# Two transformer blocks on one core: the norms of the last two heads taken by chunk ahead of the inverse of the delta rule, the next pair's factors turned a level later, and key results copied first

## The reference

```python
qkv = jax.nn.silu(causal_depthwise_conv(qkv, conv_w))
q, k, v = jnp.split(qkv, [GDN_KDIM, 2 * GDN_KDIM], axis=-1)
q = l2_norm(heads(q, GDN_DK))     # x * rsqrt(sum(x * x) + EPS), 8 heads of 128
k = l2_norm(heads(k, GDN_DK))

# gated_delta_rule, by chunk
q = q * dk ** -0.5
decay = jnp.exp(jnp.where(incl, g_cum[..., :, None] - g_cum[..., None, :], -jnp.inf))
k_beta = k * beta[..., None]
a_low = jnp.where(strict, jnp.einsum('bhncd,bhnsd->bhncs', k_beta, k) * decay, 0.0)
rhs = jnp.concatenate([v * beta[..., None], k_beta * jnp.exp(g_cum)[..., None]], axis=-1)
sol = lax.linalg.triangular_solve(eye + a_low, rhs, left_side=True, lower=True, unit_diagonal=True)
attn_intra = jnp.einsum('bhncd,bhnsd->bhncs', q, k) * decay
```

## Time and profile before

| | |
|---|---|
| median of 3 executions | 2322.6 us (2318.1 to 2330.74) |
| profiled execution | 2318.65 us, span 2316.8 us |
| mean granted clock of the PE | 0.935 of full speed |
| busy over the span | PE 88%, DVE 45%, ACT 31%, POOL 15% |
| projection and inverse in the span | 697 to 953.4 us and 953.7 to 1130.5 us |

### The profile page before, as it was taken

How to read it: one execution, slowest core, us unless ns; L and a number is a source line. 1 busy time by engine, 2 the same in 40 slices (tenths; PEclk the granted TensorE clock), 3 DMA queues, 4 the chain that set the end, 5 groups by cost and what they waited for, 6 DMA issues and landing times. The chain is left out here.

```text
span 2316.8 us, 28906 instructions
## 1 busy us (share of the span) xinstructions
PE 2038.6 (88%) x11212; PEld 1508.8 (65%) x11212; DVE 1035.5 (45%) x1493; ACT 710.1 (31%) x1118; POOL 343.9 (15%) x311
## 2 busy tenths in 40 slices
PE   5988894987767999598999999997898779999999
PEld 2766662322226777377877888885676557888887
DVE  3432434111126578646445344334497654544333
ACT  2422132110113444243324222232442653322222
POOL 1332011111112443134221000000000321000000
PEclk9999896998988999789999999998899889999999
DMA  8146026999951222000012322321221002222321
GB/s 332 51 151 235 11 73 272 376 424 423 418 234 73 91 82 91 19 2 2 2 55 77 105 91 100 96 95 55 82 75 62 0 18 84 98 94 97 99 100 46
DMA packets 61950, 283.32 MB, mean 122 GB/s; under 512 B 9984, under 2 KB 11296, under 8 KB 52512
## 3 DMA queue, kind: packets, MB, share of 16 engines
q1 hardware_dynamic: 53072, 266.95, 31.2%
q0 software_dynamic: 6256, 11.03, 1.3%
q10 hardware_dynamic: 2528, 4.01, 0.5%
HBM read 280.90 MB, written 14.68 MB: 128 GB/s over the span
## 5 line engine op out<-in xcount | busy, mean ns | idle before, releaser
L307 PE MATMUL ps<-ff_hhi,ff_whi 128*128 128x512 f32 x704 | 276.7, 393 | 8.6 <-DVE ff_hlo L2662 8.3
L308 PE MATMUL ps<-ff_hhi,ff_wlo 128*128 128x512 f32 x704 | 275.4, 391 | 0.0
L309 PE MATMUL ps<-ff_hlo,ff_whi 128*128 128x512 f32 x704 | 275.3, 391 | 0.0
L2580 DVE TENSOR_TENSOR ff_wlo<-ring,ff_whi 128x1024 fp32r<-128x1024 f32 x132 | 163.6, 1239 | 247.4 <-ACT ff_whi L2576 247.4
L2576 ACT ACTIVATE ff_whi<-ring 128x1024 fp32r<-128x1024 f32 x132 | 139.3, 1055 | 321.5 <-PE ps L309 300.0
L1451 PE MATMUL ps<-w_up,hgT 128*64 128x512 f32 x576 | 144.6, 654 | 45.9 <-DMA w_up<-experts 45.9
L307 PEld LDWEIGHTS ps<-ff_hhi,ff_whi 128*128 128x128 f32 x704 | 133.2, 189 | 38.3 <-DVE ff_wlo L2580 10.2
L308 PEld LDWEIGHTS ps<-ff_hhi,ff_wlo 128*128 128x128 f32 x704 | 133.1, 189 | 28.0 <-issue 0.5
L309 PEld LDWEIGHTS ps<-ff_hlo,ff_whi 128*128 128x128 f32 x704 | 133.0, 189 | 28.0
L307 PE MATMUL ps<-ff_ahi,ff_whi 128*128 128x512 f32 x352 | 136.9, 389 | 0.0
L308 PE MATMUL ps<-ff_ahi,ff_wlo 128*128 128x512 f32 x352 | 136.9, 389 | 0.0
(11 more groups left out here) (543 smaller groups left out, 3949.1 us busy)
## 6 DMA issues: line engine op xcount, KB each, us to landing
ring<-stream SPq DMA_DIRECT2D x276, 512.0 KB, 3.3
w_up<-experts SPq DMA_DIRECT2D x36, 2048.0 KB, 17.7
mix<-experts SPq DMA_DIRECT2D x18, 1024.0 KB, 20.9
hn<-experts SPq DMA_DIRECT2D x18, 1024.0 KB, 21.8
yrow<-y_dram SPq DMA_DIRECT2D x4, 1024.0 KB, 8.0
tab<-table POOLq DMA_DIRECT2D x1, 2528.5 KB, 12.3
res<-xT ACTq DMA_DIRECT2D x1, 2048.0 KB, 18.5
h_dram<-mix SPq DMA_DIRECT2D x4, 512.0 KB, 11.1
```

Of the source, the lines that this page charges most:

```text
L307: pe.matmul(out, w_hi, a_hi, start=start, stop=False)
L308: pe.matmul(out, w_lo, a_hi, start=False, stop=False)
L309: return pe.matmul(out, w_hi, a_lo, start=False, stop=stop)
L2580: ve.tensor_tensor(w_lo[:, j % 2, :], ring[:, (B0 + j) % SLOTS, :], w_hi[:, j % 2, :].bitcast(F32), ALU.subtract).then_inc(blocks_done, 1)
```

## The change

1. In the projection the last pair's four `sums`, `roots` and `normalise` go. In their place `late_sums` makes the sums of the squares by chunk: 16 matmuls, each with 128 x 4 weights that are one in one column, so that chunk c has its four rows (q6, k6, q7, k7) at PSUM partitions 32c to 32c + 3 of bank 2. `late_roots` takes four roots of 4 x 128 into `late`, a part of `sml`. Two constants are set on POOL early in the block.
2. In the inverse the DVE inverts `late` (128 x 128) behind its two memsets. Behind the first pair's `spread_rows` the PE spreads the rows of `late` over all partitions (`late_rows`, 16 matmuls with 4 rows and 128 columns), and behind the first pair's `difference` the DVE scales Q and K of heads 6 and 7 in eight operations of 128 x 256. `decays` and what follows on the DVE stand behind them, `pair_products` on the PE behind `late_rows`.
3. `turn_t` of the next pair moves from behind level 4 to behind level 5, ahead of `turn_kv`.
4. `keep_result` copies K's result first. The next pair's level 1 waits for K's copy ahead of its first half and for V's ahead of its second half.

```diff
         rows = tab[0:8, TABLES["rcount"]].rearrange("p (a t) -> p a t", a=4)
+        late, late_eps = sml[:, 2 * T:2 * T + P], sml[:, 2 * T + P:2 * T + P + 1]
+        hot = TABLES["hot"].start + 7
...
-                turns(pe, one_turn, lambda before: [sums(u, before) for u in range(2)])
+                def late_sums(before):
+                    pe.wait_ge(conved[0], before * 3 + 3)
+                    for n in range(4):
+                        pe.wait_ge(squared[n // 2], before * 2 + n % 2 + 1)
+                        for c in range(TT):
+                            m = pe.matmul(ps[32 * c:32 * c + 4, 2, 0:P], tab[:, hot - n:hot - n + 4],
+                                          sq[:, n // 2, n % 2, c * P:(c + 1) * P], start=n == 0, stop=n == 3)
+                    m.then_inc(late_sum, 1)
+                turns(pe, one_turn, late_sums)
...
                 for n in range(4):
                     rest_of_block(0, n)
+                pool.memset(late[:, :], 1.0).then_inc(late_set, 1)
+                pool.memset(late_eps[:, :], EPS).then_inc(late_set, 1)
...
-                turns(act, one_turn, lambda before: [roots(u, before) for u in range(2)])
+                def late_roots(before):
+                    act.wait_ge(late_set, 2)
+                    act.wait_ge(late_sum, 1)
+                    for c in range(TT):
+                        r = slice(32 * c, 32 * c + 4)
+                        act.activation(late[r, :], ps[r, 2, 0:P], ACT.Sqrt, bias=late_eps[r, :]).then_inc(late_root, 1)
+                turns(act, one_turn, late_roots)
...
-                turns(ve, one_turn, lambda before: [normalise(u, before) for u in range(2)])
+                turns(ve, one_turn, lambda before: None)
...
                         if lv == 1:
                             pe.wait_ge(S["t_copy"][u], p + 1)
-                            if p:
-                                pe.wait_ge(S["fin_kept"][u], 2 * p)
+                            if p == 0:
+                                pe.wait_ge(late_done, 4 * u + 4)
+                            else:
+                                pe.wait_ge(S["fin_kept"][u], 2 * p - 1)
...
                             if lv > 1:
                                 pe.wait_ge(S["tT_up"][u], TUPS * p + lv - 1)
+                            elif p:
+                                pe.wait_ge(S["fin_kept"][u], 2 * p)
...
+                def late_rows():
+                    pe.wait_ge(late_inv, 1)
+                    for c in range(TT):
+                        r = slice(32 * c, 32 * c + 4)
+                        for n in range(4):
+                            a = 32 * c + n
+                            m = pe.matmul(ps[:, 4 * (c // 2) + 2 + c % 2, n * P:(n + 1) * P],
+                                          tab[r, a:a + 1].to_broadcast([4, P]), late[r, :], start=True, stop=True)
+                        m.then_inc(late_back, 1)
                 both = range(2)
-                for part in (spread_rows, pair_products, turn_t, turn_kv):
+                for u in both:
+                    spread_rows(0, u)
+                late_rows()
+                for part in (pair_products, turn_t, turn_kv):
...
-                    beside = {1: spread_rows, 3: pair_products, 4: turn_t, 5: turn_kv} if p + 1 < NPAIR else {}
+                    beside = {1: (spread_rows,), 3: (pair_products,), 5: (turn_t, turn_kv)} if p + 1 < NPAIR else {}
...
-                    for n, keep in enumerate((V, K)):
+                    for n, keep in ((1, K), (0, V)):
...
-                for part in (difference, decays, read_products, first_level, keep_kd):
+                ve.reciprocal(late[:, :], late[:, :]).then_inc(late_inv, 1)
+                for u in range(2):
+                    difference(0, u)
+                for c in range(0, TT, 2):
+                    ve.wait_ge(late_back, c + 2)
+                    for n in range(4):
+                        x = (Q, K)[n % 2][:, HEADS - 2 + n // 2, c * P:(c + 2) * P].rearrange("p (b t) -> p b t", b=2)
+                        ve.scalar_tensor_tensor(x, x, (P ** -0.5, 1.0)[n % 2],
+                                                ps[:, 2 * c + 2:2 * c + 4, n * P:(n + 1) * P], ALU.mult, ALU.mult
+                                                ).then_inc(late_done, 1)
+                for part in (decays, read_products, first_level, keep_kd):
```

More of the change, by code:

```diff
@@ L1558, in program @@
         egl = sb("egl", [P, HEADS, TT], on=gdn)
+        late, late_eps = sml[:, 2 * T:2 * T + P], sml[:, 2 * T + P:2 * T + P + 1]
+        late_set, late_sum, late_root = (sem(f"late_{n}") for n in ("set", "sum", "root"))
+        hot = TABLES["hot"].start + 7
         rows = tab[0:8, TABLES["rcount"]].rearrange("p (a t) -> p a t", a=4)
@@ L1980, in program @@
         zeroed = sem("i_zeroed")
+        late_inv, late_back, late_done = (sem(f"late_{n}") for n in ("inv", "back", "done"))
         NPAIR = HEADS // 2
@@ L2085, in _ @@
                 for p in range(NPAIR):
-                    beside = {1: spread_rows, 3: pair_products, 4: turn_t, 5: turn_kv} if p + 1 < NPAIR else {}
+                    beside = {1: (spread_rows,), 3: (pair_products,), 5: (turn_t, turn_kv)} if p + 1 < NPAIR else {}
                     for lv in range(1, LEVELS + 1):
                         level(p, lv)
-                        if lv in beside:
+                        for part in beside.get(lv, ()):
                             for u in both:
-                                beside[lv](p + 1, u)
+                                part(p + 1, u)
                     for u in both:
```

## The result

| | before | after |
|---|---|---|
| median | 2321.66 us (20 executions, 2315.23 to 2342.57) | 2302.17 us (20 executions, 2296.55 to 2319.99) |
| ratio of times | 1 | 0.9917, 95% interval 0.9894 to 0.994 |
| profiled execution | 2318.65 us, span 2316.8 | 2312.3 us, span 2310.5 |
| mean granted clock | 0.935 | 0.934 |

The change saves 19.5 us by the medians, 19.3 by the ratio (13.9 to 24.6); 17.0 were forecast. So the whole spans of two profiles are not compared here; the stretch from the first record of the sums to the next stage's first matmul is, and parts of it.

The account below looks back on a forecast made before the run. Holes in the PE's row, not transfers, were taken to bound the kernel. -16.7 + 7.6 - 7.9 + 0 = -17.0 gave 2301.6 us on the profiled execution, 2305.6 with 3.95 for the median; range 2298 to 2313.

Parts of the forecast that it names:

- Part 1: Projection's tail: late sums and roots replace the old sums, roots, reciprocals and scalings; gain 16.7 us, bounds 14.3 to 17.0.
- Part 2: Inverse, first pair: late rows and multiplications ahead of the decays make them 7.6 us later; bounds 0.6 to 8.2.
- The choice of half clock: First pair's spreads and late rows: PE at 1.2 of 2.4 GHz, so late rows take 7.2 us instead of 3.8.
- Part 3: Inverse, three pairs: factors turned behind level 5 remove the PE's 2.14 us hole; gain 7.9 us, bounds 5 to 9.
- first_level ends at 1053.76 ... just in time: Pair 1: VectorE's first_level ends at 1053.76, level 5's first subtraction is due at 1053.7, so no wait.
- Rival (d): Inside level 5, VectorE's first_level becomes the wait and the turn's move gives nothing; gain 9.1, 2313.5 us; chance 0.07.
- An idle PE put down to VectorE: Sign of being wrong: the PE idles inside level 5, waiting for VectorE; no size given.
- late rows of 7 us and decays at 16: Signs of being right in the first pair: late rows take 7 us, decays start 16 us after the PE's start.
- Part 4: Pair's end, K copied first: ScalarE's four copies are the chain; gain 0, bounds 0.1 lost to 1.5 us gained.
- (a): Low ends meet: serial sums with table load behind, 8.2 back, 5 from the turn; gain 11.1, 2311.5 us; chance 0.15.
- (b): Clock stays up over spreads and late rows: cost 0.6 to 4.2 instead of 7.6; 2298.6 to 2302.2 us; chance 0.15.
- (c): Inverse's clock recovers later: nine more half-clock levels eat the gain, fifteen make it over 12 us slower; chance 0.03.

Follow-up runs that it names:

- sums in turn: Changed kernel with the late sums done chunk by chunk, so that eight records of one column group follow one another; one execution, 2315.80 us.
- the repeat: Changed kernel measured and profiled again, unedited; median 2303.07 us of 6, ratio 0.9915 to the kernel before.
- the part alone: Kernel before with only K's result copied first, and the waits that go with it; one execution, 2318.84 us.
- three and four edits: Changed kernel with GpSimd's level 6 masks held, late rows across row groups, scaling behind decays: 2298.04 us; with V copied by VectorE too: 2294.14, again 2297.94.
- the late norms alone: Changed kernel with the factors' turn back behind level 4 and V copied first again; median 2305.71 us of 10, ratio 0.9938.
- POOL's wait: Changed kernel with GpSimd's level 6 masks held until the next pair's first_level is done; median 2301.0 us of 10, ratio 0.9938.

## Why the prediction was right

**Part 1** was forecast at 16.7 and measured at 16.70. The sums at 1.1 us (1.06) held. That the table load stands behind the two waits is not settled by after, where ScalarE was busy with a silu until 953.03 and both waits were over by then; the row of the sums in turn shows it. Here it cost nothing either way. The four roots took 1.51 against 1.4.

**Part 2** was forecast at 7.6 and measured at 4.6 to 5.0 for the decays, 3.6 and 5.6 for level 1. The choice of half clock was right: 0.52 over spreads and late rows. The mis-sized term is the late rows: 0.224 each was a quarter of a 512-column spread; a record of 4 rows and 128 columns took 0.155, the 32 together 4.97 instead of 7.2. Another 0.7 is that the rows start 6.52 us after the first spread and not 7.2, and the last four multiplications came to 969.02 - 967.65 = 1.4, counted from the rows' end (962.68 + 4.97), against 1.5; together that makes decays at 12.86 instead of 15.9.

**Part 3** was forecast at 7.9. At equal clock pairs 1-2 gained 1.0, of which 0.9 is the turn; from level 5's start to the transposes of K it was 5.95 us (1056.71 - 1050.76) instead of 4.55 forecast. If these 1.40 are missing in each of three pairs, 7.9 - 4.2 = 3.7 are left; that is the forecast corrected, not a measurement. The step that failed is "first_level ends at 1053.76 ... just in time". It took that end from the trace of before, where VectorE had the time to itself. In before, GpSimd was idle just then: the PE was at the factors' turn, so level 5's first product, which GpSimd's masks for level 6 wait for, came late:

```profile
1050.50 1.28 POOL L2155 TENSOR_TENSOR Q<-Q,inv_er 128x512 f32<-128x512 f32 x1
...
1051.93 0.86 DVE L2213 TENSOR_TENSOR inv_tT<-inv_aT,tab 64x256 f32<-64x256 f32 x2
...
1052.83 0.17 DVE L2216 COPY egl<-inv_er 128x4 f32<-128x4 f32 x1
...
1055.07 2.14 POOL L2163 TENSOR_TENSOR inv_bmT<-hctx,tab 128x512 f32<-128x512 f32 x2 [3.28 <-PE ps L2006]
```

With the factors' turn behind level 5, that product follows level 4 at once, GpSimd starts at 1051.49 instead, and its masks and the scaling of Q behind them lie exactly beside `first_level`. VectorE's slowed steps end 0.27 and 0.02 us after GpSimd's. The move of one PE step thus moved another engine's work onto the step that the PE waits for. The trace of before had shown the price, in the first pair, where both engines run side by side:

```profile
970.88 1.20 POOL L2163 TENSOR_TENSOR inv_bmT<-inv_aT,tab 128x512 f32<-128x512 f32 x1 [1.09 <-DVE inv_aT L2205]
972.04 2.92 POOL L2155 TENSOR_TENSOR Q<-Q,inv_er 128x512 f32<-128x512 f32 x2
972.39 1.12 DVE L2216 COPY egl<-inv_er 128x4 f32<-128x4 f32 x1
...
976.17 0.17 DVE L2216 COPY egl<-inv_er 128x4 f32<-128x4 f32 x1
```

The same copy, 1.12 beside GpSimd and 0.17 without. I had not compared these lines. (The Trainium skill, "GPSIMD Engine Reference", Specifications, says that GpSimd shares its SBUF interfaces with VectorE and contends with its instructions in a 2-port mode or with two SBUF inputs. The trace agrees: the two-input step went from 0.86 to 2.45.)

Rival (d), that `first_level` becomes the wait inside level 5, came true in its mechanism and not in its price: it took back a half of part 3, not all. An idle PE put down to VectorE was also a sign of being wrong that the prediction had named, and it was there (1.26); late rows of 7 us and decays at 16, named as signs of being right, were not.

**Part 4** was forecast at 0 and brought 0.1 a pair, by the repeat and by the part alone. That ScalarE is the chain was half right: with two of its copies gone only 0.4 came free.

**The sum.** The stage is 21.5 shorter than before in the first profile and 14.9 in the repeat; 2.0 of the difference is in level 1, 4.5 in the stretch behind it. It goes with the clock: by the brackets, the PE was at half from the first spread to pair 2's level 6 for 44.9 us in before, 34.1 in the first profile and 51.2 in the repeat. On a straight line between the two profiles, 44.9 us would give 17.3, an estimate from three executions. By parts, 16.7 - 5.6 + 3.7 + 0.3 = 15.1 with the repeat's level 1, whose 5.6 has 9.1 us more at half clock in it. By the whole kernel's ratios, part 1 with part 2 is worth 14.4 (forecast 9.1) and part 3 4.9 (forecast 7.9), each known to some 6 us only, together the 19.3 of the change.

The median's 19.5 lies between the two stages' 14.9 and 21.5; what a usual execution gains in the stage is open. Some 4 us of it may lie in unchanged stages: behind the stage the 14 profiled executions spent between 1180.0 and 1185.6 us, before 1184.3 and both of after 1180.2, and one profile of before can't tell a lasting difference from chance. So the forecast of the total was near for parts that erred both ways: part 2 too dear by 2 to 4, part 3 too good by 4.2. That these nearly cancelled was luck; only part 1 was right to its steps.

Rivals (a), (b) and (c): sums in turn cost 1.1 and not the 2.4 that (a) wanted; the clock did not stay up (b), though the PE's pause was 3.4 us; and (c), a later recovery, came in one profile and small: from the first spread to pair 0's level 6 the clock was at half for 34.7 us in before, 27.3 in the first profile and 44.4 in the repeat. By the 6.6 us that 17.1 us more at half clock made between the two profiles, these 9.7 cost an estimated 4, not the 17 that (c) wanted.

## What to carry to other kernels

When a step is moved, list what it released and what its new neighbour releases on every engine: here a PE step moved by one level, and GpSimd's masks came to lie on VectorE's step that the PE waits for. Take a duration from a row with the same neighbours, and look in the trace for the same instruction with another duration; that is what contention looks like before it is tried. And where the clock falls and rises within a stage, compare distances with equal time at half clock, not stage totals.

## What the hardware showed that was not expected

**A busy PE at half clock for some 38 us.** The first block's attention (L802 to L828), far ahead of the change and the same code in both kernels, by stretches, first before, then the first profile of after:

```profile
235.00:275.00 40.00, 37.50 (x314) 28.53 (x314) 13.74 (x21) 6.73 (x14) 1.80 (x1) 0.88 0.06 16
```

```profile
235.00:275.00 40.00, 37.88 (x246) 34.17 (x248) 7.49 (x17) 1.97 (x6) 1.80 (x1) 0.52 0.05 16
```

The groups by line in 240 to 280, again before and then after (line, engine, operation, names, shapes, count | busy us, mean ns | idle):

```profile
L822 PE MATMUL ps<-qb,SS 64*128 64x64 f32 x128 | 9.0, 280 | 0.0
```

```profile
L822 PE MATMUL ps<-qb,SS 64*128 64x64 f32 x128 | 15.8, 424 | 0.0
```

The PE was busy for 37.88 of 40 us at a mean clock of 0.52. The seam of this execution comes at 951.73 instead of 932.59, and the kernel with sums in turn, whose clock there was 0.58, has it at 946.96. In the other twelve profiles the sums start between 932.6 and 937.4. This accounts for the long profiled execution of after: against the repeat the seam is 17.7 later (934.04 there) and the stage 6.6 shorter, 11.1 of the 11.2 us between the two; that it also makes the long ones among the unprofiled executions of either kernel is likely from their distance of some 15 us, not shown. (The Trainium skill, "TensorE: Matmul & The Clock Gate", Part 1, has the clock rise with a busy PE; this stretch disagrees.)

**The clock in the pairs.** Each pair's spreads bring half clock for 3.4 or 6.8 us. All profiles of the kernels with three and four edits have 6.8 in both pairs. That costs 1.6 us a pair (40.33 at 6.8 with the late norms alone against 38.76 at 3.4 before) and gives back what POOL's wait had gained. What in those kernels brings it was not found.

**VectorE's small copy.** 128 x 4 elements, 0.17 us alone and 1.13 beside GpSimd: not only steps with two tensor inputs are held.
